# Heads in pairs in a sparse softmax, and normalising work in another order

## The reference

```
y_a = stick_breaking_attention(sa_q, sa_k, sa_v)             # 8 heads of 64
y_b = causal_softmax_attention(q_b, k_b, v_b, 96 ** -0.5)    # "mla": 8 heads of 64 + 32, q_b and k_b
                                                             # normalised per head and rotated
y_c = dsa_attention(rms_norm(ds_q), rms_norm(ds_k), ds_v, ix_q, ix_k, ix_w, positions, rel_bias)
branches = stack([y_a * silu(z_a), y_b * silu(z_b), y_c * silu(z_c)])
x = x + sum(sigmoid(g + gate_b) * (branches @ w_branch)) @ w_out
```

## Time and profile before

| what | value |
|---|---|
| three runs | 1429.9, 1406.52, 1426.58 us, median 1426.58 us |
| the profiled execution | 1419.21 us, its span 1417.5 us |
| mean granted TensorE clock | 0.97 of full speed |

### The profile page before, as it was taken

The page is one execution under the profiler, slowest core; times in us unless marked ns, Lnnn a source line. Parts: engine busy times, 40 slices in busy tenths (PEclk is TensorE's granted clock), DMA queues, the critical chain, the costliest instruction groups (busy, mean ns, idle before and its releaser), DMA issues.

```text
span 1417.5 us, 17812 instructions
## 1 busy us (share of the span) xinstructions
PE 1327.0 (94%) x6538; PEld 988.4 (70%) x6538; DVE 775.8 (55%) x1582; ACT 608.2 (43%) x1130; POOL 181.8 (13%) x302
## 2 busy tenths in 40 slices
PE   3589999889999999999999999988999999999998
PEld 2278766645557888888878876655555788888887
DVE  7856677767643334454446577677844233335442
ACT  3335556666563223233333455566645322323330
POOL 3400212123330000000000021112333000000000
PEclk9899999999999999999999999999979999999999
DMA  6432112100240322223231311210014033222331
GB/s 163 127 97 89 60 61 45 31 30 2 75 134 31 119 89 89 90 89 119 89 90 60 106 44 60 45 46 15 25 51 132 32 98 110 90 89 89 110 98 60
DMA packets 118423, 109.14 MB, mean 77 GB/s; under 512 B 34496, under 2 KB 101056, under 8 KB 118336
## 3 DMA queue, kind: packets, MB, share of 16 engines
q1 hardware_dynamic: 110096, 107.96, 25.3%
q10 hardware_dynamic: 8240, 0.03, 0.3%
HBM read 100.64 MB, written 7.34 MB: 76 GB/s over the span
## 4 chain that ended last, share of the span: by engine, by line
PE 78%; DVE 10%; ACT 5%; issue 3%; POOL 2%; SPq 1%; DMA 0%; ACTq 0%; DVEq 0%; POOLq 0%
PE bank L722 20%; PE bank L724 19%; PE bank L723 19%; PE bank L1020 4%; PE bank L988 3%; PE bank L829 2%; PE bank L1002 2%; PE bank L981 2%; DVE w_lo L631 2%; PE bank L853 1%; POOL reach L457 1%; PE bank L843 1%; PE bank L990 1%; DVE score L1600 1%; ACT w_hi L625 1%
## 5 line engine op out<-in xcount | busy, mean ns | idle before, releaser
L722 PE MATMUL bank<-h_hi,w_hi 128*128 128x512 f32 (+1 forms) x928 | 362.8, 391 | 10.2 <-DVE ds_q L1609 5.7
L723 PE MATMUL bank<-h_lo,w_hi 128*128 128x512 f32 (+1 forms) x928 | 354.3, 382 | 0.0
L724 PE MATMUL bank<-h_hi,w_lo 128*128 128x512 f32 (+1 forms) x928 | 354.3, 382 | 0.0
L631 DVE TENSOR_TENSOR w_lo<-raw,w_hi 128x2048 fp32r<-128x2048 f32 (+2 forms) x98 | 188.1, 1919 | 142.5 <-ACT w_hi L625 142.2
L722 PEld LDWEIGHTS bank<-h_hi,w_hi 128*128 128x128 f32 x928 | 176.5, 190 | 54.4 <-issue 8.5
L625 ACT CAST w_hi<-raw 128x2048 fp32r<-128x2048 f32 (+2 forms) x100 | 159.4, 1594 | 120.3 <-PE bank L724 120.3
L723 PEld LDWEIGHTS bank<-h_lo,w_hi 128*128 128x128 f32 x928 | 176.7, 190 | 33.9 <-issue 2.9
L724 PEld LDWEIGHTS bank<-h_hi,w_lo 128*128 128x128 f32 x928 | 176.7, 190 | 33.7
L1406 ACT ACTIVATE gate<-bank,gains 128x512 f32<-128x512 f32 x48 | 33.0, 688 | 166.1 <-PE bank L724 166.1
L1892 POOL TENSOR_SCALAR probs<-probs,stat 128x128 f32<-128x128 f32 (+3 forms) x128 | 74.5, 582 | 181.1 <-DVE stat L1711 175.4
L722 PE MATMUL bank<-br_hi,w_hi 128*128 128x512 f32 x192 | 74.7, 389 | 0.0
(11 more groups left out here) (218 smaller groups left out, 2327.3 us busy)
## 6 DMA issues: line engine op xcount, KB each, us to landing
raw<-in_w_in SPq DMA_DIRECT2D x56, 1024.0 KB, 5.2
raw<-in_w_branch SPq DMA_DIRECT2D x12, 1024.0 KB, 5.2
raw<-in_w_out SPq DMA_DIRECT2D x8, 1024.0 KB, 5.1
bias<-bias_dram SPq DMA_DIRECT2D x16, 256.0 KB, 2.9
bias<-bias_dram SPq DMA_DIRECT2D x16, 192.0 KB, 2.6
x_sb<-in_x SPq DMA_DIRECT2D x4, 512.0 KB, 4.9
bias_dram<-bias_out SPq DMA_DIRECT2D x8, 256.0 KB, 2.9
raw<-in_w_in SPq DMA_DIRECT2D x4, 512.0 KB, 4.6
```

The lines of the kernel that those rows point to most:

```text
L631: e.tensor_tensor(w_lo[:, s % RING, a:b], raw[:, s % RAW, a:b], w_hi[:, s % RING, a:b].bitcast(F32), ALU.subtract).then_inc(*lo_signal(nam ...
L722: pe.matmul(out_ap, lh, rh, start=start and i == 0, stop=False)
L723: pe.matmul(out_ap, lh, rl, start=False, stop=False)
L724: mm = pe.matmul(out_ap, ll, rh, start=False, stop=stop and i == n - 1)
```

## The change

In the sparse softmax the units go by pairs of heads: step j (16 of them) has block t = j % 4 of heads 2p and 2p + 1. Both scores are issued, then both masks; the transposes are those of step j - 2, the products with the values those of step j - 3. The scores use four banks (0 to 3), the copied transposes a ring of four (`probs_dsa`), the bias is loaded and waited for per unit. The first weight tile of the next stage (`z0_0`) is projected in two parts between the last steps, and the halves of `z0_0` and `z0_1` are split at steps 3, 5, 7 and 9. In the latent softmax `prep_k(h + 1)` stands ahead of the first score of head h and `prep_q(h + 2)` behind the transposes; `sq_k` stands ahead of the exponential. In the stick-breaking steps the factor (`rs_of`) stands ahead of `rounded` and the second half of a split, and `normed` ahead of the split and of two steps of the search. At the end of that stage `prep_k(0)` stands behind `norm_q(0)`, and `prep_q(1)` ahead of `norm_k(0)`. The two additions of `k_rope` go to index unit 16, and at the seam of the layers both `h_lo_of` calls stand behind the third row block.

```
+def dsa_units(j):
+    return [(N_MLA + 2 * j + o, o, 2 * (j // ST) + o, j % ST) for o in range(2)]
 # SP: the bias
-for h in range(HEADS):
-    if h >= 2: e.wait_ge(*row_max.at(N_SOFT // 2 + 4 * (h - 2) + ST - 1))
...
+for j in range(DSA_STEPS):
+    for u, o, h, t in dsa_units(j):
+        if j >= ST: e.wait_ge(*row_max.at(u - 2 * ST))
+        e.dma_start(bias[:, o, OFF[t]:OFF[t] + P * (t + 1)], bias_dram[h, ...]).then_inc(*bias_in[o][t].tick(h, by=16))
 def s_bank(u):
-    return bank[2 + u % S_RING]
+    return bank[2 + u % S_RING] if u < N_MLA else bank[(u - N_MLA) % 4]
 # TensorE, in s_of
+if u >= N_MLA + 4:   pe.wait_ge(*row_max.at(u - 4))
+elif u >= N_MLA:     pe.wait_ge(*probs_exp.at(N_MLA - 1 if u % 2 else N_MLA - 2))
...
+for j in range(DSA_STEPS + DSA_AV):                      # DSA_T, DSA_AV = 2, 3
+    if j < DSA_STEPS:
+        for u, o, h, t in dsa_units(j): s_of(u)
+        for u, o, h, t in dsa_units(j): chosen_of(u)
+    for i in (N_MLA + 2 * j, N_MLA + 2 * j + 1): mla_tail(i)
+    if 0 <= j - DSA_STEPS < 2:
...
+        mm = project("z0_0", "z0_0", 0, P, part=j - DSA_STEPS)
+    if 0 <= j - DSA_T < DSA_STEPS:
+        for u, o, h, t in dsa_units(j - DSA_T): t_of(u)
+    if 0 <= j - DSA_AV < DSA_STEPS: values_of(j - DSA_AV)
+def values_of(j):
+    for u, o, h, t in dsa_units(j):
+        pe.wait_ge(*turned_copied(u))
+        if t == 0 and o == 0:
+            pe.wait_ge(*(y_out["dsa"].at(h // 2 - 1) if h else y_out["mla"].at(3)))
...
 # ScalarE
+for j in range(DSA_STEPS + DSA_AV + 1):
+    if j < DSA_STEPS:
+        for u, o, h, t in dsa_units(j): exp_of(u)
...
+    if 0 <= j - DSA_T < DSA_STEPS:
+        for u, o, h, t in dsa_units(j - DSA_T):
+            e.wait_ge(*probs_turned.at(u))
+            e.wait_ge(*pv_done.at("soft", turned_before(u)))
+            e.copy(turned(u), t_bank(u)[:, 0:P * (t + 1)])
+    if j >= DSA_AV + ST and (j - DSA_AV) % ST == 0:
+        pair = (j - DSA_AV) // ST - 1
+        pair_out("dsa", pair, N_MLA + 8 * pair + 7)
+    if j in SPLIT_Z: split_hi(e, *SPLIT_Z[j])
 # VectorE: as before per unit, for both units of step j, then the latent copies, then
+    for u, o, h, t in dsa_units(j): inverse(u)
+    if j - 1 in SPLIT_Z: split_lo(e, *SPLIT_Z[j - 1])
 # TensorE, latent
+    if i and t == 0 and h + 1 < HEADS: prep_k(h + 1)
     s_of(i)
-    if t == 0: prep_k(h + 1)
-    if t == 2 and h + 2 < HEADS: prep_q(h + 2)
     t_of(i - 3)
+    if t == 2 and h + 2 < HEADS: prep_q(h + 2)
 # ScalarE, stick-breaking steps
-    rounded(i); split_part(i, 1); rs_of(tile, ...)
+    rs_of(tile, ...); rounded(i); split_part(i, 1)
 # VectorE, stick-breaking steps
-    rest(i); split_part(i, 1); topk_step(4 * i + 2); topk_step(4 * i + 3); normed(tile, ...)
+    rest(i); normed(tile, ...); split_part(i, 1); topk_step(4 * i + 2); topk_step(4 * i + 3)
```

More of the change, by code:

```diff
@@ L653, in turned_before @@
             br, h, t = soft_units[u]
+            if br == "dsa":
+                return u - 4 if u >= N_MLA + 4 else N_MLA - 1
             if h % 2 == 0:
@@ new lines, in pair_out @@
+                def pair_out(br, pair, u):
+                    e.wait_ge(*pv_done.at("soft", u))
+                    e.copy(y[:, 4 + pair, :] if br == "mla" else y_dsa[:, pair, :], bank[Y][:, :]).then_inc(*y_out[br].tick(pair))
+                for i in range(N_MLA):
+                    if i > AV_LAG and (i - AV_LAG - 1) % 8 == 7:
+                        pair_out("mla", (i - AV_LAG - 1) // 8, i - AV_LAG - 1)
+                    br, h, t = soft_units[i]
+                    if t == 0 and h + 1 < HEADS:
+                        sq_k(h + 1)
+                    exp_of(i)
+                    if i < 2:
+                        for s in (2 * i, 2 * i + 1):
+                            e.wait_ge(*dense.at(f"v_b{s}"))
+                            e.copy(v_b[:, s, :], t_bank(s)[:, :]).then_inc(*act_evac.tick(f"v_b{s}"))
+                    if h + 1 < HEADS:
+                        if i == 0:
+                            rs_q(1)
+                        if t == 1:
+                            rs_k(h + 1)
+                        if t == 2 and h + 2 < HEADS:
+                            sq_q(h + 2)
+                        if t == 3 and h + 2 < HEADS:
+                            rs_q(h + 2)
@@ L1824, in _ @@
                                     xn_of(done)
-                            if s in SEQ[2:]:
-                                h_lo_of(SEQ[SEQ.index(s) - 2])
+                            if s == SEQ[2]:
+                                for done in SEQ[:2]:
+                                    h_lo_of(done)
                             layer.l -= 1
```

275 lines of the change are left out of this document (149 added, 126 removed).

## The result

The change makes no gain. Its 20 runs have a median of 1427.65 us (1422.5 to 1429.6), the 20 runs of the kernel before beside them 1426.58 us (1401.1 to 1432.3), and the ratio is **1.014, 95% interval 1.012 to 1.016**: slower by 1.4%, within the 2% that count as no change. The medians stand only 1 us apart because the kernel before varies with the clock, and the ratio compares only those runs of it that stay within 1.5% of its fastest. The means over all 20 runs, 1420.5 and 1427.0 us, are 0.5% apart. The forecast was 1404 us.

What follows compares the result with a forecast made beforehand. TensorE was taken to bound the kernel, and a chain through ScalarE and VectorE the new sparse stage. 1419.2 us profiled + 2.1 sparse - 17.3 other edits = 1404 us; its own range 1392 to 1418, the overall range 1380 to 1434.

Steps and rivals of the forecast that it cites:

- `k_rope` and `h_lo`: Index queries and layer seam: `k_rope` gains 1.4 us, twice, 2.8 us; `h_lo` gains 2.1 us once.
- Sparse stage: Sparse softmax: 70.8 us a stage, 4.1 more than in layer 0, 2.0 less than in layer 1, together 2.1 more.
- the three waits: Sparse softmax, between pairs: TensorE idles about 3.5 us for bank Y's copy; 1.9 us lost each, 5.8 us a layer.
- the credit for `z0_0`: Sparse softmax: 24 products of `z0_0` done there take 5.3 us off the next stage.
- Rival 1: Sparse softmax: the clock holds, both layers lose 6.7 us less, 1391 us; chance 0.20.
- rival 2: Sparse softmax: the chain doesn't bind, TensorE at its own pace, stage 49.0 us, kernel 1360 us; chance 0.08.
- rival 3: Sparse softmax: half clock for the whole stage, some 95 us, kernel 1452 us; chance 0.07.
- Half clock at idle stretches: Sparse softmax: each of three idle stretches brings 7 us of half clock, 6.7 us lost in a layer.
- The end of stick-breaking: End of stick-breaking: `prep_k(0)` moves into the wait for the factors, first latent score 1.8 us earlier.
- The steps of stick-breaking: Stick-breaking steps: VectorE's earlier normalisation shrinks a wait of 2.83 us by 1.1; one step gets 0.2 us worse.
- Latent softmax: Latent softmax: four waits of up to 1.07 us for `k_sq` go, 3.5 us gained, twice, 7.0 us.
- Rival 4: Reordered normalisations don't pay, each wait replaced by the next behind it: 1421 us; chance 0.15.

Runs made afterwards that it cites:

- e3: The whole change with ScalarE copying bank Y at the start of its step, ahead of the exponentials: 1403.4 us, ratio 0.995 to the kernel before.
- e5: The whole change with 15 unread multiplications on TensorE in each wait between pairs, bank Y still copied late: 1414.9 us, ratio 1.000 to the kernel before.
- e6: The change with bank Y and transposes copied ahead of exponentials (1386.3 us), end of stick-breaking put back to its old order: 1383.1 us.
- e7: The change with bank Y and transposes copied ahead of exponentials (1386.3 us), key head's norm put ahead of the second query tile: 1380.8 us.
- e8: The change with bank Y and transposes copied ahead of exponentials (1386.3 us), steps of stick-breaking put back to their old order: 1384.1 us.
- e13: The whole change, sparse softmax untouched, with the key head's norm ahead of the second query tile and the old stick-breaking steps: 1415.4 us, ratio 1.000.
- e9: The change with bank Y and transposes copied ahead of exponentials (1386.3 us), latent softmax put back to its old order: 1393.1 us.
- e10: The change with bank Y and transposes copied ahead of exponentials (1386.3 us), `k_rope` and `h_lo` put back to their old places: 1388.8 us.
- e2: The whole change without its sparse part, the sparse softmax going unit by unit as before: 1419.2 us, ratio 1.006 to the kernel before.
- e14: The kernel before with only the change's stick-breaking part, its steps and its end: 1416.6 us, ratio 1.003 to the kernel before.

## Why the prediction was wrong, step by step

Against its own baseline the forecast was -15 us of span and the trace shows +10. The 25.6 us lie in these steps (trace minus forecast): 1.0 in the sparse stages with `z0_0`, 13.5 in stick-breaking, 6.2 in the latent stages and 4.8 in `k_rope` and `h_lo`.

- **Sparse stage, right.** Pairs of scores, the three waits and their clock were forecast at 70.8 us a stage after the credit for `z0_0`. Measured: 75.7 and 77.7 less 5.4 for `z0_0`, 70.3 and 72.3. The terms that can be read held: 3.5 us of idling forecast, 3.8 to 4.3 measured; 1.9 us lost for each wait, 11.5 / 6 = 1.9 by e3 and e5; 7 us of half clock costing 2.2 us, 6 us costing 2.1 by e5; 5.3 us of credit, 5.4 measured. From one pair to the next it took 15.6 to 16.8 us (400.04 to 415.95, and so on), where these terms give 17.2, so a part of the agreement is cancelling. Rival 1 fell, for the clock did not hold; rival 2, for no stage came under 70 us; and rival 3, for the stages were at 0.86 and 0.82 of the clock and not at half.
- **Half clock at idle stretches, right.** The Trainium skill's warning that short idling between groups of matmuls makes the clock swing ("TensorE: Matmul & The Clock Gate", "A second HAM failure mode: psum-queue depth-cycling") fits two runs here. e5 removes the idling between pairs alone and raises the clock from 0.964 to 0.977, though those idle stretches, 3.8 to 4.3 us, are not short. In e3 the longest are 2.0 to 2.6 us, and its sparse stages ran at 0.90.
- **Its baseline, wrong for the ratio.** The forecast compared with 66.7 and 72.8 us as if they were the stage's cost. They are draws from 60.4 to 72.8 us. The change has half clock at each of its waits in the trace, and none of its 20 runs has a mean clock above 0.969, so it lost the fast draws. That is why medians 1 us apart go with a ratio of 1.014. The three times of the kernel before (1406.5 beside 1426.6 and 1429.9 us) said that such draws exist, and the forecast did not ask what a stage costs at full clock. A wait doesn't always bring half clock: in the trace before, the wait of 0.83 us at the start of the sparse stage of layer 0 was followed by full clock, and the same wait in layer 1 (0.82 us, at 1036.79) by 10.3 us of half clock from 1039.2 on, one of the three cases that the forecast put down to waits of 0.93 us.
- **The end of stick-breaking, wrong (-1.8 us forecast).** `prep_q(1)` was taken to fill the wait for the factors. It waits itself, for `q_head`, and the key head's norm is behind it. Putting the old end back gives 1.7 us of stick-breaking in each layer, and 1.6 us of the latent stage behind it (e6); one swap gives as much (e7).
- **The steps of stick-breaking, wrong (1.1 us less in one step, 0.2 more in another).** The 1.2 us at 242.62 are there. The search that moved behind the norms then delays `q_head` by 0.7 us, the next `ds_q` comes 0.3 us later, and the waits for `stick_a`, which the forecast did not name, grow by 2.8 us a layer. Putting the steps back gains 2.9 and 1.7 us of stage (e8). The forecast followed the norm forwards and not what was pushed back. With the end, stick-breaking went +4.6 and +3.5 us for -2.7 forecast: 13.5 of the 25.6 us. With both mended it takes 142.7 us, 1.2 and 2.2 less than in the kernel before (e13).
- **Latent softmax, a size that was off in this kernel: 6.2 of the 25.6 us.** The waits fell from 1.07 to 0.42 us, not to nothing, and the stage gains 2.3 us (e9) for 3.5 forecast. In the whole change 1.4 us of one stage and 2.5 of the other went back, for with stick-breaking mended they are 69.5 us (e13). The wait of 3.11 us ahead of them is followed by half clock (298.20:301.60 at 0.58). Rival 4 said that the other edits would give nothing, since each wait is replaced by the next. They cost 7 us by the trace, and its reason holds for a part: `k_sq`, `q_head` and `xn` are such waits, `stick_a` is not.
- **`k_rope` and `h_lo`, wrong: 4.8 us.** `k_rope` gave 1.4 us and cost 0.5. At the seam `h_lo` of both blocks came early, and TensorE then waited 3.55 us for `xn` of the third block instead of 2.18 us for `h_lo`, with 6.9 us of half clock from 751.6 on (3.4 us in the trace before). VectorE gets to this `xn` only behind a weight split of 2.29 us that starts at 748.74; in the trace before that stood under the products which `h_lo` had held up. e10 puts both edits at zero at equal clock. What would bring this `xn` forward was not tried.

Open: why e2 had no run above a clock of 0.972, when e14, with the same end of stick-breaking and the same sparse list, had runs up to 0.985. The line of time and clock accounts for the times, not for what sets the clock in the one and not in the other. Open too is what e5 loses at equal clock.
